# Decays of an SSD scan: one-hot products of transposed running sums in place of masked-matrix products

## What is computed

```python
    a_cum = jnp.cumsum(dtr * a.reshape(ng, rep), axis=2)
    xdt = xr * dtr[..., None]
    seg = a_cum[:, :, :, None] - a_cum[:, :, None, :]
    tri = jnp.tril(jnp.ones((chunk, chunk), bool))[:, :, None, None]
    decay = jnp.exp(jnp.where(tri, seg, -jnp.inf))
    cb = jnp.einsum('bclgn,bcsgn->bclsg', cr, br)
    y_diag = jnp.einsum('bclsgr,bcsgrp->bclgrp', cb[..., None] * decay, xdt)
...
    y_off = jnp.einsum('bclgn,bcgrpn->bclgrp', cr, h_prev) * jnp.exp(a_cum)[..., None]
```

## Time and profile before

| | before |
|---|---|
| median of the three runs | 1794.22 us |
| span of the profiled execution | 1797.8 us |
| PE busy in that span | 1478.2 us, 82% |
| DVE, ACT, POOL busy | 653.7, 461.2, 187.4 us |
| mean granted TensorE clock (1 is 2.4 GHz, 0.5 is 1.2 GHz) | 0.889 |
| the scan: first and last instruction on DVE, ACT, POOL or PE | about 599.0 to 730.8 us |

### The profile page before, as it was taken

How to read it: one execution, slowest core, us unless ns; L and a number is a source line. 1 busy time by engine, 2 the same in 40 slices (tenths; PEclk the granted TensorE clock), 3 DMA queues, 4 the chain that set the end, 5 groups by cost and what they waited for, 6 DMA issues and landing times. The chain is left out here.

```text
span 1797.8 us, 25386 instructions
## 1 busy us (share of the span) xinstructions
PE 1478.2 (82%) x10279; PEld 1084.0 (60%) x10279; DVE 653.7 (36%) x1268; ACT 461.2 (26%) x804; POOL 187.4 (10%) x314
## 2 busy tenths in 40 slices
PE   4999789868889677699489988838999839988865
PEld 1999444455579333599355544438999826554435
DVE  3322265543236565652611111143246451111104
ACT  3221255532234532421301100132224221110012
POOL 0000033210000233000011110020000001111102
PEclk8999799889989777699689999957999969999985
DMA  7222587549822601420989999841222298999964
GB/s 288 71 94 71 223 321 273 219 178 371 320 76 68 221 1 58 141 78 17 372 328 389 376 392 401 321 154 35 83 94 96 92 409 324 380 391 399 393 223 149
DMA packets 133593, 399.73 MB, mean 222 GB/s; under 512 B 15842, under 2 KB 67682, under 8 KB 110690
## 3 DMA queue, kind: packets, MB, share of 16 engines
q1 hardware_dynamic: 114370, 359.01, 53.2%
q10 hardware_dynamic: 11488, 21.24, 3.3%
q0 software_dynamic: 7616, 17.84, 3.1%
HBM read 368.72 MB, written 37.19 MB: 226 GB/s over the span
## 5 line engine op out<-in xcount | busy, mean ns | idle before, releaser
L2855 PE MATMUL ex_gups<-ex_gu,ex_he 128*64 128x256 f32 x1728 | 210.1, 398 | 43.3 <-DMA ex_gu<-in_moe_w_up 40.4
L2855 PEld LDWEIGHTS ex_gups<-ex_gu,ex_he 128*64 128x64 f32 x1728 | 126.2, 143 | 111.1 <-DMA ex_gu<-in_moe_w_up 44.9
L2900 DVE TENSOR_TENSOR ex_hid<-ex_sg,ex_gups 128x128 f32<-128x128 f32 x64 | 18.4, 288 | 299.7 <-ACT ex_sg L2924 299.7
L2873 PE MATMUL ex_yps<-ex_dn,ex_hid_t 128*64 128x512 f32 x512 | 123.9, 604 | 0.9 <-issue 0.9
L2833 POOL DMA_INDIRECT ex_hg<-h_rows,route_tok x64 | 60.2, 941 | 508.8 <-PE ex_trps L2845 425.1
L225 PE MATMUL sc_ps<-h_hi,sc_hi 128*128 128x272 f32 x352 | 101.7, 289 | 0.5 <-PEq L3111 0.5
L225 PE MATMUL sc_ps<-hT_r,sc_hi 128*128 128x272 f32 x352 | 100.9, 287 | 0.0
L225 PE MATMUL sc_ps<-h_hi,sc_w_r 128*128 128x272 f32 x352 | 100.7, 286 | 0.0
L2924 ACT ACTIVATE ex_sg<-ex_gups 128x128 f32<-128x128 f32 x64 | 17.8, 278 | 301.1 <-PE ex_gups L2855 301.1
L2914 ACT ACTIVATE ex_yo<-ex_yps 128x512 f32<-128x512 f32 x64 | 38.2, 597 | 184.8 <-PE ex_yps L2873 184.8
L2893 DVE COPY ex_he<-ex_trps 128x512 f32<-128x512 f32 x64 | 44.3, 692 | 64.7 <-PE ex_trps L2845 64.7
(11 more groups left out here) (535 smaller groups left out, 3400.3 us busy)
## 6 DMA issues: line engine op xcount, KB each, us to landing
ex_dn<-in_moe_w_down SPq DMA_DIRECT2D x64, 1024.0 KB, 26.6
ex_gu<-in_moe_w_gate SPq DMA_DIRECT2D x54, 1024.0 KB, 24.6
ex_gu<-in_moe_w_up SPq DMA_DIRECT2D x54, 1024.0 KB, 26.6
ada_rest_w<-in_ada_w SPq DMA_DIRECT2D x40, 1024.0 KB, 6.5
as_pages<-in_cache_kT SPq DMA_DIRECT2D x32, 512.0 KB, 6.5
as_pages<-in_cache_v SPq DMA_DIRECT2D x32, 512.0 KB, 5.7
y_rows<-ex_yo ACTq DMA_DIRECT2D x128, 128.0 KB, 7.0
qkv_w<-in_mix_w_in SPq DMA_DIRECT2D x12, 1024.0 KB, 5.3
```

The costliest lines, as they stand in the source:

```text
L2855: last = nc.tensor.matmul(gu_ps[64 * q:64 * q + 64, :, :], he[n % 2][:, j, :], ex.gu[n % S][:, :, j, q * P:(q + 1) * P], start=(j == 0), s ...
L2873: last = nc.tensor.matmul(y_ps[n % 2][64 * c:64 * c + 64, :], hid_t[:, m * CAP:(m + 1) * CAP], ex.dn[n % S][:, m, c * 512:(c + 1) * 512], ...
L2900: nc.vector.tensor_tensor(hid[:, :], sg[:, :], gu_ps[:, 1, :], ALU.mult).then_inc(done["hid"], 1)
```

## The change

The reference's running sum is now made once for all chunks, and transposed: PE multiplies `dA_twice` (each head's column of dA twice, at columns 0 to 15 and 32 to 47, with zeros between) by `tri_le` for each of the four chunks, into `ss_seg` (48 partitions, 512 columns). ACT rounds it to the reduced float32 type F32R in `run_T` (partitions 0 to 31) and in `run_hi` (partitions 32 to 47); DVE writes what the rounding left off into partitions 32 to 47 of `run_T`. A product with a column of `pick`, which has a one at head h and at 32 + h, broadcast over 128 columns, then gives both parts' sum on all partitions. Per unit `ss_bc` is four such products of 128 columns, and `ss_seg` is one product of the identity with -1e30 above the diagonal (`above_r`, 512 columns) and four such products added onto it. The missing -a_cum[s] comes in as the bias of the exponential, from `run_neg`; so `dec` takes four instructions of 128 columns in place of one of 512. All these products are F32R. In chunk 0, `ss_bc`, `e_t` and its product with C are left out. `spread` and `ss_mat` are gone. The sample unit keeps its two float32 products.

```diff
+        run_T = k.sb("ss_runT", [48, TP], F32R, ctx=ctx)
+        dA_twice = k.sb("dA_twice", [P, 4, 48], ctx=ctx)
...
                 nc.tensor.matmul(ac_ps[0:TS, 64:80], gt_same[:, :], dA[0:TS, 4, :], start=True, stop=True)
+                nc.tensor.matmul(ac_ps[:, 288:352], k.tri_le[:, :], dA[:, 0:4, :], start=True, stop=True)
...
+                pe.wait_ge(s["pick"], 2)
+                for c in range(4):
+                    last = nc.tensor.matmul(seg_ps[0:48, c * P:(c + 1) * P], dA_twice[:, c, :], k.tri_le[:, :], start=True,
+                                            stop=True)
+                last.then_inc(s["aT_mm"], 1)
...
+                    if c:
+                        if i > FIRST_E:
+                            pe.wait_ge(s["e"], i - FIRST_E)
+                    elif i == 0:
+                        pe.wait_ge(s["aT"], 2)
...
-                    nc.tensor.matmul(bc_ps[:, :], ones, m, start=True, stop=True).then_inc(s["sums"], 1)
...
+                    def running(dst, h, start):
+                        return nc.tensor.matmul(dst[:, h * P:(h + 1) * P],
+                                                pick[:, 4 * q + h:4 * q + h + 1].to_broadcast([48, P]),
+                                                run_T[:, c * P:(c + 1) * P], start=start, stop=True, skip_group_check=True)
+                    if c:
+                        for h in range(4):
+                            last = running(bc_ps, h, True)
+                        last.then_inc(s["sums"], 1)
                     if i:
                         pe.wait_ge(s["decx"], i)
-                    nc.tensor.matmul(seg_ps[0:TS if c == 4 else P, :], above, m, start=True, stop=True)\
-                      .then_inc(s["sums"], 1)
+                    nc.tensor.matmul(seg_ps[:, :], ident_r[:, :], above_r[:, :].unsqueeze(1).to_broadcast([P, 4, P]),
+                                     start=True, stop=False, skip_group_check=True)
+                    for h in range(4):
+                        last = running(seg_ps, h, False)
+                    last.then_inc(s["segs"], 1)
...
+                V.tensor_tensor(run_T[32:48, :], seg_ps[32:48, :], run_hi[32:48, :], ALU.subtract).then_inc(s["aT"], 1)
...
-                    for h in range(4):
-                        nc.scalar.activation(mat[:, n % 2, h, :], k.tri_le[:, :], ACT.Copy,
-                                             scale=dA[:, c, 4 * q + h:4 * q + h + 1]).then_inc(s["mat"], 1)
...
+                    for h in range(4):
+                        last = nc.scalar.activation(dec_of(i)[:, h, :], seg_ps[:, h * P:(h + 1) * P], ACT.Exp,
+                                                    bias=run_neg[:, c, 4 * q + h:4 * q + h + 1])
+                    last.then_inc(s["decx"], 1)
...
+                nc.scalar.activation(run_neg[:, :, :], ac_ps[:, 288:352].rearrange("p (c h) -> p c h", h=H), ACT.Copy,
+                                     scale=-1.0).then_inc(s["aexp"], 1)
+                act.wait_ge(s["aT_mm"], 1)
+                nc.scalar.activation(run_hi[32:48, :], seg_ps[32:48, :], ACT.Copy).then_inc(s["aT_lo_in"], 1)
+                nc.scalar.activation(run_T[0:32, :], seg_ps[0:32, :], ACT.Copy).then_inc(s["aT"], 1)
...
-                    pool.wait_ge(s["e"], i + 1)
+                    if c == 0:
+                        return
+                    pool.wait_ge(s["e"], i - FIRST_E + 1)
```

More of the change, by code:

```diff
@@ L1463, in phase_ssd @@
         bank_no["update", b] = 5 + b if b < 3 else 6 + b
-    names = ("made", "tr", "trc", "dA", "ac_mm", "aexp", "own_d", "xdt", "xw", "cb", "cbc", "mat", "mat4", "sums",
+    names = ("made", "tr", "trc", "dA", "ac_mm", "aexp", "own_d", "xdt", "xw", "cb", "cbc", "mat4", "sums", "segs",
              "e", "decx", "m", "cs", "y", "yo", "sload", "stored", "bm", "skip4", "decayed", "oc", "masked", "own_p",
-             "zeroed", "turned", "upper")
+             "zeroed", "turned", "upper", "pick", "aT_mm", "aT_lo_in", "aT")
     s = {n: k.sem("ss_" + n) for n in names}
@@ L1487, in phase_ssd @@
         gt_same = k.sb("gt_same", [TS, TS], ctx=ctx)
-        mat = k.sb("ss_mat", [P, 2, 4, P], ctx=ctx)
+        run_T = k.sb("ss_runT", [48, TP], F32R, ctx=ctx)
+        dA_twice = k.sb("dA_twice", [P, 4, 48], ctx=ctx)
+        pick_f, pick = k.sb("ss_pickf", [48, H], ctx=ctx), k.sb("ss_pick", [48, H], F32R, ctx=ctx)
+        run_neg = k.sb("ss_runneg", [P, 4, H], ctx=ctx)
+        ident_r, above_r = k.sb("ss_ident_r", [P, P], F32R, ctx=ctx), k.sb("ss_above_r", [P, P], F32R, ctx=ctx)
+        above_f = nc.alloc_sbuf_tensor_at("ss_above_f", [P, P], F32, offset=k.offset["hT"] + 16384)
         mat4 = k.sb("ss_mat4", [TS, H, TS], ctx=ctx)
@@ L1495, in phase_ssd @@
         om = k.sb("ss_om", [P, 8, HD], ctx=ctx)
+        run_hi = nc.alloc_sbuf_tensor_at("ss_runhi", [48, TP], F32R, offset=k.offset["ss_om"])
         oc = k.sb("ss_oc", [P, ROUNDS, 2, HD], ctx=ctx)
@@ L1906, in _ @@
                   .then_inc(s["made"], 2)
+                own.did(nc.gpsimd.memset(dA_twice[:, :, 16:32], 0.0))
+                own.step(nc.gpsimd.memset(pick_f[:, :], 0.0))
+                for first in (0, 32):
+                    own.step(nc.gpsimd.affine_select(out=pick_f[:, :], in_=pick_f[:, :], pattern=[[-1, H]], base=-first,
+                                                     channel_multiplier=1, compare_op=ALU.not_equal, fill=1.0))
+                nc.gpsimd.tensor_copy(pick[:, :], pick_f[:, :]).then_inc(s["pick"], 1)
+                own.step(nc.gpsimd.memset(above_f[:, :], 0.0))
+                own.step(nc.gpsimd.affine_select(out=above_f[:, :], in_=above_f[:, :], pattern=[[1, P]], base=0,
+                                                 channel_multiplier=-1, compare_op=ALU.is_ge, fill=NO_WAY))
+                own.did(nc.gpsimd.tensor_copy(above_r[:, :], above_f[:, :]))
+                own.did(nc.gpsimd.tensor_copy(ident_r[:, :], k.ident[:, :]))
+                pool.wait_ge(s["dA"], 1)
+                own.did(nc.gpsimd.tensor_copy(dA_twice[:, :, 0:16], dA[:, 0:4, :]))
+                own.settle()
+                nc.gpsimd.tensor_copy(dA_twice[:, :, 32:48], dA[:, 0:4, :]).then_inc(s["pick"], 1)
                 nc.gpsimd.memset(zeros[:, :], 0.0).then_inc(s["zeroed"], 1)
```

53 lines of the change are left out of this document (25 added, 28 removed).

## The result

The change made the kernel slower: 1816.62 us in the median of 4 runs against 1796.33 for the kernel before (with a fourth run beside the three), ratio 1.0115, 95% interval 1.009 to 1.014. Forecast were 1789.1 us and a range to 1799.

What follows compares the result with a forecast made beforehand. PE was taken as full early in the scan, then waiting for a DVE and POOL queue. 1.4 us gained by unit 7 plus 3.7 later gave 5.1 us: 1792.7 us profiled, 1789.1 us median, range 1781 to 1799 us.

Steps and rivals of the forecast that it cites:

- The read of the bound: Scan: PE is full in chunks 0 and 1; later it waits for DVE and POOL multiplies sharing one queue.
- The products: Each unit from chunk 1: 1.1 us of PE against 1.7 at the upper clock, 2.25 against 3.6 at the lower.
- one-hot products at 0.2 us: Sign that the forecast is wrong: one-hot products in the scan taking 0.2 us each at the upper clock.
- The exponentials: Each unit's dec: four instructions take 1.13 us against 0.60, covered from chunk 1 on by POOL's e_t product.
- Term 1: Prologue: first x_tok copy 2.8 us later, first dec ends at 614.1 instead of 612.4, so 1.7 us later.
- Chunk 0: First four units take 9.9 us from 614.1, so unit 5 starts at 624.0, 1.3 us earlier than before.
- Term 2: Unit 4's outputs: they start at 627.0 after a wait for the queue, 0.5 us ahead of before.
- Terms 3 and 4: Units 5 to 7: sample's product 1.4 us ahead; units 8 to 16: 3.7 us more.
- The clock falls: slower: Between units 1 and 7 PE gets the lower clock; the kernel becomes 8 us slower, near 1802 us; chance 0.13.
- a clock of 0.5 between 615 and 637: Sign that the forecast is wrong: a granted clock of 0.5 in that stretch of the scan.

Runs made afterwards that it cites:

- e6: e1 with dec's exponential of each prompt unit split into four ACT instructions of 128 columns with a bias: 1782.03 us, ratio to before 0.9939.
- e15: e7 with the changed kernel's prologue products on PE and its two ACT copies added, results unread: 1790.05 us, ratio to before 0.9952.
- e18: e7 with 36 unread ACT copies of 14 columns delaying the first x_tok copy, PE idle: 1790.94 us, ratio to before 0.9978.
- e7: e1 with ss_bc, e_t and its product with C also left out in chunk 0: 1779.86 us, ratio to before 0.9894.
- e5: e1 with each F32R decay-sum product cut into four of 128 columns, a weight load each: 1802.11 us, ratio to before 1.0022.
- e1: Kernel before with masked matrix, ones and tri_gt in F32R, so the large decay-sum products take one pass: 1784.93 us, ratio 0.9937.
- e13: e12 with each unread product replaced by seven one-pass F32R products of 128 columns, same places and busy time: 1785.75 us, ratio to before 0.9932.
- e12: e7 with 20 unread two-pass float32 products of 512 columns put into PE's waits: 1769.00 us, ratio to before 0.9834.
- e14: e12 with each unread product replaced by three one-pass F32R products of 512 columns, same places: 1776.65 us, ratio to before 0.9892.
- e10: Changed kernel with running sums, one-hot weights, identity and mask table in bfloat16 instead of F32R: 1796.30 us, ratio to before 0.9997.

## Why the prediction was wrong

**The read of the bound** held: PE's waits after are those named (`cbs` 5.55, `ss_om` 4.4, `mixT` 4.3 us, as the earlier trace rows). The sample's product still waits for `cbs`:

```profile
655.99 0.42 PE L1583 MATMUL ss_acps<-xc 128*32 128x32 f32 x4 [5.55 <-DVE cbs L1743]
```

**The products.** Mis-sized. 0.11 us for 128 columns and 0.23 for 512 came from back-to-back rows in attention; here it is 0.145 and 0.43. A unit costs 1.6 us, not 1.1, so 0.1 is saved at the upper level and 0.8 at the lower, not 0.6 and 1.3. Each of the 16 prompt units thus saves 0.3 to 0.5 us less than forecast, part of which lies in PE's waits: on that alone, by my estimate, the forecast of 5.1 us faster goes to about no change. The mark "one-hot products at 0.2 us" wasn't reached, but 0.145 was enough.

**The exponentials.** Right: 1.14 us for four (1.13 forecast), and free by e6. `weigh`, with chunk 0 free of `e_t`, has a mean of 1.26 us (1.45 before).

**The prologue, Term 1.** Right in place: the four products last 1.94 us, POOL's `pick` is in time, the first `dec` ends at 615.40, 613.9 on the clock of the kernel before, for 614.1:

```profile
605.53 1.94 PE L1563 MATMUL ss_seg<-tri_le,dA_twice 128*48 128x128 f32 x8
...
614.26 1.14 ACT L1896 ACTIVATE dec<-ss_seg,ss_runneg 128x128 f32<-128x128 f32 x4 [2.11 <-PE ss_seg L1605]
```

Wrong in price: it counts once in the sum, where e15 and e18 show about 10 us for it or for half of it. Both stand on e7, with wide products; on the changed kernel the price wasn't measured.

**Chunk 0 and Term 2.** This is the step that failed first. Unit 5's products start at 630.01, 628.5 when the scan's later start (1.5 us) is taken off, in place of 624.0. The 9.9 us for chunk 0 were counted at the upper level; the profile after has 0.50 from 610 to 620 with PE 9.06 of 10 us busy, where the same stretch of before reads

```profile
610.00:620.00 10.00, 10.00 (x46) 5.07 (x45) 4.10 (x5) 7.26 (x18) 3.82 (x3) 0.94 0.92 326
```

The upper level came at about 611 before; after, it came at about 623, with PE busy without a break from 617:

```profile
611.00:612.00 1.00, 1.00 (x6) 0.56 (x5) 0.00 (x0) 0.38 (x2) 0.76 (x1) 0.94 0.53 186
```

```profile
622.00:623.00 1.00, 1.00 (x2) 0.08 (x1) 0.16 (x1) 0.00 (x0) 0.00 (x0) 0.50 1.09 385
623.00:624.00 1.00, 1.00 (x9) 0.77 (x10) 0.53 (x1) 0.06 (x1) 0.00 (x0) 0.88 0.92 327
```

Term 2 put unit 4's outputs at 627.0. They start at 634.71, 633.2 by the same count, behind a wait of 3.02 us for unit 4's `weigh`, which lasts 2.81 us beside POOL's `e_t` times C of unit 5 (631.71, 1.25 us) and `skip4` (632.93, 0.60 us):

```profile
631.28 2.81 DVE L1757 TENSOR_TENSOR dec<-dec,cbs 128x512 f32<-128x512 f32 x1
```

```profile
634.71 0.70 PE L1642 MATMUL ss_y<-dec,xdt 128*64 128x128 f32 x4 [3.02 <-DVE dec L1757]
```

```profile
634.00:636.00 2.00, 1.29 (x12) 1.32 (x14) 2.00 (x7) 0.00 (x0) 0.00 (x0) 0.50 0.00 0
```

A wait there was forecast (some 1.9 us, from 625.1 to 627.0), a change of level wasn't: the clock was at 0.50 again from about 634 to 643.

**Terms 3 and 4.** The sample's product starts 9.3 us later than before, not 1.4 earlier; the scan ends 20.6 us later, not 5.1 earlier. Both terms took each unit's level over from the profile of before, as if it belonged to the stretch. In this kernel the same stretches were granted other levels.

**The rival that came true** is "The clock falls: slower", in mechanism and first place: its mark, a clock of 0.5 between 615 and 637, is there up to about 623 and again from about 634. Its price was 8 us, because I let the fall end at unit 7 and had "the rest of the scan" give back 3.6. It didn't end: after 660 PE is 9 to 10 us busy in most stretches and mostly at 0.50. Its chance of 0.13 rested on 700:710, which held 1.00 with PE 7.63 us busy; the profile after shows 0.50 with PE 9.06 and 8.62 of 10 us busy, so that row was no evidence of what this kernel would be granted. The profile of before itself spoke against reading the level off the busy share, in rows that the prediction left out:

```profile
690.00:700.00 10.00, 8.34 (x15) 3.07 (x17) 3.87 (x13) 1.03 (x2) 1.41 (x2) 0.51 0.00 0
...
710.00:720.00 10.00, 10.00 (x28) 3.77 (x28) 4.00 (x4) 1.20 (x2) 3.12 (x2) 0.66 0.65 264
```

The Trainium skill's rule that activity releases the level ("TensorE: Matmul & The Clock Gate", "What's actually happening") pointed this way. The trace agrees only in part: the level fell, but PE's busy share of the scan rose, from 108 of 135 us to 130 of 155, so busy time as the profile counts it doesn't tell which level is granted.

Summed: the replaced products -7.3 us of busy time, the prologue's 1.9 + 0.7, the untouched work in the four groups shown +22.3 and in the smaller ones (transposes, the sample's sums and so on) +5.6: 23.2, against PE's +22.2, since neighbouring products overlap. That cutting four-byte products to 128 columns comes with more time at the lower level is shown by e5 against e1; e13 against e12 and e14 support it, and e10 ties it to the four-byte type. Whether it is the columns or their weight loads, and by what rule the chip grants the level, no run here shows. That a late start costs time is shown by e18 on e7's kernel; the share of each in the 20 us is not.

## What to carry to other kernels

Before trading one wide product for several of 128 columns on a partly busy PE, price the work that isn't changed at the lower clock too: here it lost three times what the new products saved. Where float32 accuracy allows, the plain step (one F32R pass of the same wide products, 11 us faster) is better than the clever one. Once PE has waits, a wide product that nobody reads may be worth putting there (11 us in the medians, e7 to e12, with intervals that just overlap); the narrow ones of e13 gained nothing.
